# Two transformer blocks on one core: 32 pairs of weight pieces with seven block products in place of eight

## The reference

```
h = h + stick_breaking_mixer(rms_norm(h, norm_mix), sb_w_qkv) @ sb_w_o
h = h + square(relu(rms_norm(h, norm_mlp) @ mlp_w1)) @ mlp_w2
x = rms_norm(h, final_norm)
...                                            # second block: w_in, attention, pooling, w_o
up = causal_dwconv(rms_norm(x, pre_ffn_g) @ w_up)
y  = (gelu(up[..., :5632]) * up[..., 5632:]) @ w_down
x  = x + rms_norm(y, post_ffn_g)
```

## Time and profile before

| | |
|---|---|
| median of 3 runs | 2097.33 us (2096.52 to 2098.95) |
| the profiled execution | 2095.49 us, span 2093.8 us |
| PE busy | 2083.5 us, 9304 matmuls |
| DVE busy | 1224.2 us (58%) |
| ACT busy | 1072.2 us (51%) |
| POOL busy | 119.7 us (6%) |
| DMA | 469.46 MB, mean 224 GB/s |

### The profile page before, as it was taken

The page is one execution under the profiler, slowest core; times in us unless marked ns, Lnnn a source line. Parts: engine busy times, 40 slices in busy tenths (PEclk is TensorE's granted clock), DMA queues, the critical chain, the costliest instruction groups (busy, mean ns, idle before and its releaser), DMA issues.

```text
span 2093.8 us, 23749 instructions
## 1 busy us (share of the span) xinstructions
PE 2083.5 (100%) x9304; PEld 1728.1 (83%) x9304; DVE 1224.2 (58%) x1312; ACT 1072.2 (51%) x1303; POOL 119.7 (6%) x66
## 2 busy tenths in 40 slices
PE   9999999999999999999999999999999999999998
PEld 8888888888888888888888888888888888888887
DVE  6546556655554555455566755566666654566665
ACT  7555654555434543455455554455555533555553
POOL 3000000000000000000002000000112100011120
PEclk9999999999999999999999999999999999999999
DMA  8688666888667885688588777667878766787863
GB/s 297 197 251 236 191 188 216 260 248 235 211 193 206 241 254 194 196 243 238 192 270 232 229 244 232 197 203 211 249 236 250 220 211 193 223 247 242 251 221 121
DMA packets 291903, 469.46 MB, mean 224 GB/s; under 512 B 18512, under 2 KB 82128, under 8 KB 291280
## 3 DMA queue, kind: packets, MB, share of 16 engines
q1 hardware_dynamic: 290928, 463.46, 72.5%
q10 hardware_dynamic: 864, 4.49, 0.6%
HBM read 432.75 MB, written 35.13 MB: 223 GB/s over the span
## 4 chain that ended last, share of the span: by engine, by line
PE 96%; DVE 1%; DMA 1%; ACT 1%; issue 0%; SPq 0%; ACTq 0%; DVEq 0%
PE ps L1546 96%; DMA T<-passed_strip 1%; DVE Wl L1204 0%; DVE zs L1416 0%; ACT Wh L986 0%; DMA E<-passed_rows 0%; DVE T L1256 0%; DMA gains<-in_gains_dram 0%; DVE E L1416 0%; ACT zs L1125 0%; SPq L917 0%; DMA passed_rows<-xN 0%; ACT T L1044 0%; DVE aHL L1307 0%; PE ps L1549 0%
## 5 line engine op out<-in xcount | busy, mean ns | idle before, releaser
L1204 DVE TENSOR_TENSOR Wl<-raw,Wh 128x1024 fp32r<-128x1024 f32 x743 | 908.2, 1242 | 674.2 <-ACT Wh L986 673.6
L1546 PE MATMUL ps<-Wh,aHL 128*128 128x512 f32 x3712 | 1148.8, 390 | 2.4 <-DVE Wl L1204 0.8
L986 ACT ACTIVATE Wh<-raw 128x1024 fp32r<-128x1024 f32 x743 | 768.0, 1054 | 611.1 <-PE ps L1546 608.7
L1546 PEld LDWEIGHTS ps<-Wh,aHL 128*128 128x128 f32 x3712 | 696.8, 188 | 147.9 <-DVE Wl L1204 1.3
L1546 PE MATMUL ps<-Wl,aHL 128*128 128x512 f32 x1856 | 722.1, 389 | 0.0
L1546 PE MATMUL ps<-Wh,hid 128*128 128x512 f32 x1728 | 532.8, 389 | 0.0
L1546 PEld LDWEIGHTS ps<-Wl,aHL 128*128 128x128 f32 x1856 | 348.4, 188 | 71.8
L1546 PEld LDWEIGHTS ps<-Wh,hid 128*128 128x128 f32 x1728 | 324.3, 188 | 67.4
L1546 PE MATMUL ps<-Wl,hid 128*128 128x512 f32 x864 | 336.1, 389 | 0.0
L1546 PEld LDWEIGHTS ps<-Wl,hid 128*128 128x128 f32 x864 | 162.2, 188 | 33.7
L1546 PE MATMUL ps<-Wh,oHL 128*128 128x512 f32 x512 | 159.0, 390 | 0.0
(11 more groups left out here) (167 smaller groups left out, 687.4 us busy)
## 6 DMA issues: line engine op xcount, KB each, us to landing
raw<-in_mlp_w_dram SPq DMA_DIRECT2D x256, 512.0 KB, 4.5
raw<-in_w_up_dram SPq DMA_DIRECT2D x176, 512.0 KB, 4.6
raw<-in_sb_w_qkv_dram SPq DMA_DIRECT2D x93, 512.0 KB, 5.2
raw<-in_w_down_dram SPq DMA_DIRECT2D x88, 512.0 KB, 4.7
raw<-in_w_in_dram SPq DMA_DIRECT2D x64, 512.0 KB, 4.8
passed_strip<-T SPq DMA_DIRECT2D x104, 256.0 KB, 4.5
T<-passed_strip SPq DMA_DIRECT2D x208, 128.0 KB, 5.2
raw<-in_sb_w_o_dram SPq DMA_DIRECT2D x32, 512.0 KB, 5.4
```

The lines of the kernel that those rows point to most:

```text
L986: e.activation(Wh[:, i % NW, :], rawv[:, i % NRAW, :], ACT.Copy).then_inc(st["hi"][0], 1)
L1204: e.tensor_tensor(Wl[:, i % NW, :], rawv[:, i % NRAW, :], Wh[:, i % NW, :].bitcast(F32), ALU.subtract).then_inc(st["lo"][0], 1)
L1546: return e.matmul(o, l, r, start=start, stop=stop, skip_group_check=True)
```

## The change

In 32 places the piece of strip a and the piece of strip b with the same 256 weight rows are taken together. Tokens (2 rows of 128), weight rows (2 k-tiles) and columns (2 strips) make a 2x2 by 2x2 block product, done with seven block products for eight (the scheme of Strassen in Winograd's form). The groups are: 2 in the second pair of `sb_w_o`, 3 in each of the six pairs of `mlp_w2`, and 3 in each of the four pairs of `w_down_2`.

- On PE a group is four pieces s0 to s3 of 6, 6, 6 and 3 matmuls: 21 in place of 24. The four pieces take four places of the ring, s2 and s3 without a load of their own. Four of the seven products go to all four banks of `ps2`, the other three straight to the strips' sets; so b's set is opened at the first group, after two pieces of a.
- Weight sums, each 128x512: POOL makes `wsum0 = a0 + b0` and, in place, `b0 += b1`; DVE makes `wsum1 = wsum0 + b1` and `wsum2 = wsum1 + a1`. Pieces s1, s2 and s3 are split from them.
- Token sums, once for each k-piece that a group uses (`mix_tokens`): four DVE operations, a high part on ACT, a low part on DVE, into an area `..Mix`.
- Behind the last group of a pair a `fold` brings `ps2` into `xN` or `xn`: one ACT copy, and 8 DVE operations (5 in the first chunk of `w_down_2`), all 128x512. Strips add their own set after it.
- A ReLU strip is scaled by its factor when staged (ACT L1042), so `add_products` needs no factor and a square of the factor goes.
- Between groups stand two plain pieces each: a0 a1 G1 p p G2 p p G3, then the rest of a and b.
- The scratch for DMA descriptors is made smaller, which gives room to `wsum` and the `..Mix` areas.

```
-            i = strip_pair("w_down_2", ..., 0 if s4 else 2, "hid2", hid_tiles, [evac_y(c, s4), evac_y(c, s4 + 1)], koff=2 * at)
+            i = strip_pair("w_down_2", ..., koff=2 * at,
+                           sevens=tuple(range(2 * at, 2 * at + 3)), fold=fold_into("xn", s4, lambda: [], fresh=c == 0))
...
+        plain = [kp for kp in ks if kp not in sevens]
...
+        b[0]["first"], b[0]["start"] = False, (False, True)
+        rest = a[2:n] + b[:n]
+        p.pieces[first:] = a[:2]
+        for m, kp in enumerate(sevens):
+            seven(w, s4, kp, mov, tiles, (a[0]["strip"], b[0]["strip"]), koff, m, m == 0, fold if m == len(sevens) - 1 else None)
+            p.pieces += rest[2 * m:2 * m + 2] if m < len(sevens) - 1 else rest[2 * m:]
+        p.pieces += a[n:] + b[n:]
...
+    def sums_and_split(i):
+        q, n = p.pieces[i], int(p.pieces[i]["kind"][1])
+        if n == 0:
+            made = {m: done("weights_added_pool" if m % 2 else "weights_added") for m in (1, 3, 2, 4)}
+            step("weight_sums", a=raw_of[i] % NRAW, b=raw_of[i + 1] % NRAW, need=[landed(i), landed(i + 1), *free["sums"]], made=made)
+            free["sums"] = [(lo_sem, i + 4)]
+            for m in (1, 2, 3):
+                p.pieces[i + m]["made"] = made[(3, 2, 4)[m - 1]]
+        step("split", i=i, part=q["kind"], ..., loaded=landed(i) if n == 0 else q["made"], used=(mm_sem, i - NW + 1), ...)
...
 # VectorE
+                elif k == "weight_sums":
+                    e.wait_ge(*made[1])
+                    e.tensor_tensor(wsum[:, 1, :], wsum[:, 0, :], b[:, 1, :], ALU.add).then_inc(made[2][0], 1)
+                    e.wait_ge(*made[2])
+                    e.tensor_tensor(wsum[:, 2, :], wsum[:, 1, :], a[:, 1, :], ALU.add).then_inc(made[4][0], 1)
 # GpSimd
+                elif k == "weight_sums":
+                    for t in st["need"]:
+                        e.wait_ge(*t)
+                    e.tensor_tensor(wsum[:, 0, :], a[:, 0, :], b[:, 0, :], ALU.add).then_inc(made[1][0], 1)
+                    e.wait_ge(*made[1])
+                    e.tensor_tensor(b[:, 0, :], b[:, 0, :], b[:, 1, :], ALU.add).then_inc(made[3][0], 1)
 # TensorE
+                terms = {"s0": (("a11", side[:, 0, :], ...), ("a12", a[:, 0, :], ...)),
+                         "s1": (("d1", side[:, 2, :], ...), ("d3", b[:, 0, :], ...)),
+                         "s2": (("d0", side[:, 1, :], ...), ("d2", side[:, 3, :], ...)),
+                         "s3": (("a22", a[:, 1, :], ...),)}[q["kind"]]
```

More of the change, by code:

```diff
@@ L90, in strip, with strip_pair @@
             p.pieces.append(dict(src=src, shape=2, mov=mov, kt=2 * (kp - koff), tiles=tiles, kind="N", first=n == 0,
-                                 last=n == len(ks) - 1, evac=evac, early=None, strip=strips[0]))
+                                 start=(n == 0, n == 0), last=n == len(ks) - 1, evac=evac, early=None, strip=strips[0]))
         return first
-    def strip_pair(w, s4, ks, tail, mov, tiles, evacs, koff=0):
-        first, n = len(p.pieces), len(ks) - tail
+    def strip_pair(w, s4, ks, tail, mov, tiles, evacs, koff=0, sevens=(), fold=None):
+        plain = [kp for kp in ks if kp not in sevens]
+        first, n = len(p.pieces), len(plain) - tail
@@ new lines, in strip_pair @@
+        b[0]["first"], b[0]["start"] = False, (False, True)
[5 more added lines that the diff above has]
+        p.pieces += a[n:] + b[n:]
+        order = [q["strip"] if q["kind"] == "N" else 0 for q in p.pieces[first:]]
@@ new lines, in strip_pair, with seven @@
+        assert max(j for j, k in enumerate(order) if k == 0) < max(j for j, k in enumerate(order) if k == a[0]["strip"])
+        assert min(j for j, k in enumerate(order) if k == 0) < min(j for j, k in enumerate(order) if k == b[0]["strip"])
+        return first
+    def seven(w, s4, kp, mov, tiles, pair, koff, m, opens, fold):
+        for i, kind in enumerate(("s0", "s1", "s2", "s3")):
+            src = (w, "rows", kp * 256, (s4 + i) * STRIP) if i < 2 else None
+            p.pieces.append(dict(src=src, shape=2, mov=mov, kt=2 * (kp - koff), tiles=tiles, kind=kind, m=m, first=False,
+                                 opens=opens, last=False, evac=None, early=None, strip=None, pair=pair,
+                                 fold=fold if i == 3 else None, closes=fold is not None))
@@ L293, in f @@
             free[f"set{s}"] = [lo]
+            if blk == 1 and g == 0:
+                free[f"set{s}"] = [lo, mix_tokens("oHL1", "values", 0, 2, [lo])]
             oHL_tiles[4 * g:4 * g + 4] = [lo] * 4
@@ L729, in plan_program @@
         if q["kind"] == "P":
+            assert not taken
             need += free["set2"]
+        elif q["kind"] == "s0":
+            if q["opens"]:
+                now[0] = 1 - now[0]
+                set_of[q["pair"][1]] = now[0]
+                need += free[f"set{now[0]}"] + free["set2"]
+                taken.append(i)
+            need.append(mixed_tokens[q["mov"], q["m"]])
         elif q["first"]:
@@ L741, in plan_program @@
                 need.append(tok)
-        q["set"], q["n"] = 2 if q["kind"] == "P" else set_of[q["strip"]], i
+        q["n"] = i
+        q["set"] = 2 if q["kind"] == "P" else [set_of[n] for n in q["pair"]] if q["kind"][0] == "s" else set_of[q["strip"]]
         if i < N - HELD:
```

240 lines of the change are left out of this document (186 added, 54 removed).

## The result

The changed kernel takes **2143.9 us** (median of four, 2140.8 to 2150.3) against 2096.9 on the same chip: ratio 1.0227, interval 1.0200 to 1.0253. It is 47 us slower; the forecast was 28 slower. The profiled execution took 2150.25 us, the longest of the four, and its span is 54.7 us longer than before.

What follows compares the result with a forecast made beforehand. PE's instruction stream was taken as the bound. -21.8 + 24 + 8 + 2 + 9 + 6 + 1 = +28.2 us on the profiled 2095.5 gave 2123.7, with the median 1.8 above: 2125.5 us; 8-of-10 range 2093 to 2146.

Steps and rivals of the forecast that it cites:

- The saving: On PE, 32 groups with 3 matmuls less in each, 96 x 0.2267: -21.8 us.
- The waits: PE waiting for late low splits at the groups and token sums: some 50 us, half at the `w_down_2` chunk starts.
- The chain at the start of `w_down_2`: First pairs, last strips' turnings delay splits: s3 at 27.6, next plain piece at 32.1, 11.7 late; +24 us for two pairs.
- 2.7 us at s2 of the first group: First pairs of `w_down_2`: s2's split behind a turning, ready at 10.9, wanted at 8.2; PE waits 2.7 us.
- The clock: Rival: ten new waits each lose 1.5 us at half rate, 2140 us; longer stretches 2160; chance 0.05.
- The fold: Behind a pair's last group, 5.5 us of DVE plus an ACT copy while four plain pieces are ready: 0.
- First pairs of `mlp_w2`: Three pairs, s3 ready at 22, wanted at 19.7, with late sums of group 3: +9 us.
- Token sums: In `w_up_2`, `mix_tokens` makes the split behind the gated one late, two chunks: +6 us, 0 to 6.
- GpSimd beside DVE: POOL and DVE don't run side by side, so POOL's 2.56 us a group are DVE's too: 8.1 us a group.
- ring holds: Rival: last strips' reads land early and the 2.5 us cover suffices, only the saving left: 2075.5 us; chance 0.07.
- short waits: Rival: quick reads and POOL always in DVE's gaps, waits 21 us, about the saving: 2097 us; chance 0.14.
- Everything at its upper end: Rival: all waits at their upper figures, POOL and DVE excluding each other at each sum, 69 us: 2145; chance 0.12.

Runs made afterwards that it cites:

- nine undisturbed groups: Changed kernel with groups only in both first-chunk pairs of `mlp_w2` (first group five pieces later) and the second chunk's second pair: 2089.3 us, ratio 0.9970.
- that run: Changed kernel with only the three groups of the last pair of `mlp_w2`, no token sums but those of `mlp_w1`: 2111.0 us, ratio 1.0070.
- the run with the sums alone: Changed kernel without any group, token sums made but not used: 2106.6 us, ratio 1.0043.
- the two with repeated splits: Kernel before, low split of ten pieces of `mlp_w1` made eight or ten times more: 2154.0 us (1.0273) and 2177.1 us (1.0397).
- 21 groups: Changed kernel, groups only in five `mlp_w2` pairs (first pairs' first groups later) and second pairs of `w_down_2`, its token sums seven pieces later: 2095.9 us, 0.9999.
- later first groups: Changed kernel, first group 5 or 3 plain pieces later in the five first pairs of `mlp_w2` and `w_down_2`: 2148.6 us, ratio 1.0244.
- with the token sums moved: Changed kernel without groups, token sums made but not used, those of `w_up_2` seven pieces later: 2099.6 us, ratio 1.0015.

## Why the forecast was right in direction and short in size

- **The saving**: 96 matmuls off at 0.2267. Right; nine undisturbed groups gave 7.0 us (3.8 to 8.6) for 6.1.
- **The waits**: 50 forecast, 47 measured as idle time and 52 from start to start, which is how the forecast counted. The chain at the start of `w_down_2` came 1.2 to 1.4 us later than drawn and the pairs cost 10.2 and 9.8 us for 12. One wait there was for another reason: I had 2.7 us at s2 of the first group, but the group's first piece opens the second strip's PSUM set, which was still being staged (L1167, 3.6 and 2.3 us). Waits of 3.7, 1.5 and 2.0 us stand at places that I had put at nothing (`w_in_2`, `mlp_w1`, behind the last fold); `mlp_w2`'s first pairs came out cheaper, so the good total is in part luck.
- **The clock** is the step that failed. I had a rival for it, priced at 1.5 us behind each of ten waits and put at 0.05 *instead of* the forecast. It belongs in the sum as a term: the profiled execution has nine stretches at 1.2 GHz up to its last matmul, 48 us long, and its matmuls lost 18 us in them, 2.0 us a stretch. Of the 26.5 us by which its span outgrew the forecast, that is the most; 2 are waits, and 6 the matmuls at full clock between and behind them, for which I had no term either. In the four runs the granted clock is 0.988 to 0.993 (0.999 before), and the times go in the same order, so the other three lost less.
- **What I missed**: the wait in `w_in_2`, 3.7 + 3.4 us. Groups take work out of *both* strips of a pair, so in the last pair the first strip ends 7 plain pieces before the pair's end and not 10: its turning comes 3 x 2.72 = 8.2 us later against the matmuls. (The text on record for that run has 7 and 5 pieces; the program has 10 and 7.) The rows below show it, before and after. The pair ends three pieces (8.2 us) ahead of the transposes' place, at 1080.1 before and 1092.5 after. Before, the turning started 8.2 us ahead of that; after, at the very end, and the last strip's adds stand behind it. The same shift, of two pieces, stands behind the 1.5 us in `mlp_w1`, which are gone in the run where `sb_w_o` has no groups. I priced the pairs and not what stands behind them.

```profile
1071.87 1.25 DVE L1296 STREAM_TRANSPOSE T<-E 128x1024 f32<-128x1024 f32 x1 [2.94 <-DMA E<-passed_rows]
...
1085.94 1.29 DVE L1292 TENSOR_TENSOR xN<-xN,QK 128x512 f32<-128x512 f32 x2
...
1088.23 1.03 PE L1549 MATMUL ps<-ident,xN 128*128 128x128 f32 x8
```

```profile
1092.96 1.25 DVE L1463 STREAM_TRANSPOSE T<-E 128x1024 f32<-128x1024 f32 x1 [2.64 <-DMA E<-passed_rows]
...
1103.44 1.28 DVE L1459 TENSOR_TENSOR xN<-xN,QK 128x512 f32<-128x512 f32 x2
...
1104.83 1.94 PE L1726 MATMUL ps<-ident,xN 128*128 128x128 f32 x8 [3.55 <-DVE xN L1459]
```

- **The fold**: put at 0, 2.0 us at the very last pair, where the last strips' adds and squares stand behind it; 0 in the run with nine groups.
- **First pairs of `mlp_w2`**: 9 forecast, 4.2 + 1.7. The last turnings started 4.3 to 7.2 us behind the loads and not the 9 I had allowed.
- **Token sums**: 6 forecast, 6.4 measured beside groups, and 7.7 in the run with the sums alone, where the clock fell too and the whole came to 10.
- **GpSimd beside DVE**: right. The Trainium skill (SBUF — State Buffer, Who interferes with whom) says that of a DVE instruction with two SBUF inputs and a GpSimd one that reads SBUF, whichever issues second blocks for the whole of the other. The runs agree on the side of DVE, whose splits took 1.275 us on average beside GpSimd's sums and 1.239 when these were gone.

The rival *ring holds* falls with the waits, *short waits* too. *Everything at its upper end* gave 2145, close to the result, but for the wrong reason: the waits stayed at 47 and not 69. *The clock* had the reason, and 2140 us from ten stretches of 1.5 us each.

## What to carry to other kernels

When the bottleneck engine runs from a ring counted in pieces, a change that shortens some pieces shortens the cover of everything scheduled by piece count: list what stands within a ring's length on either side, and what the stretch behind was counting on. Price a long wait of PE (3.3 us and more here) as itself plus what the clock takes behind it, 2 us each here, as a term of the sum and not as a rival. A saving of 0.68 us a group is worth taking only where nothing else falls: nine groups gained 7 us, thirty-two lost 47.

## What the hardware showed that I had not expected

- Every single wait of PE of 3.3 us and more, 21 of 21 in the traces of the changed kernel and of the two with repeated splits, came with a stretch at 1.2 GHz of 3.4, 6.8 or (once) 10.2 us, and nothing between. In the changed kernel all four such stretches began inside the wait, 1.2 to 2.4 us before PE went on. Of the waits from 1.8 to 3.2 us some brought 3.4 us at 1.2 GHz (1.85 at 361.6, 2.30 at 2024.0) and others none (1.91 at 1473.9, 2.88 at 422.5, 3.20 in the run with the token sums). Behind two of 1.2 and 1.6 us, with 1.0 us of matmuls between them, the clock fell as well, and one of 1.8 at 1053.9 with one of 1.0 close behind brought 6.8 us.
- The times spread more. The kernel before ran within 2094 to 2099 us; those with waits near 2 us ran from 2088 to 2101 (21 groups) and from 2141 to 2154 (later first groups), the slowest of 21 groups at a granted clock of 0.997 and the fastest at 0.999. The clock is not all of it: with the token sums moved, ten runs at 0.999 throughout spread from 2095 to 2103. What spreads those stays open.
